# A long convolution's parts placed between panels and heads, a short one halved in PSUM, four low halves on VectorE

## The reference

```
proj = u @ w_in                       # u = x * (1 + scale) + shift
a_in, a_gate, b_in, b_gate, q_lat, kv_lat, k_rope, c_gate, merge_logits = split(proj)
a1, a2 = split(a_in);  a = a1 * sigmoid(a2)
a = causal_depthwise_conv(a, conv_a_w) + conv_a_b          # 31 taps, 512 channels
a = silu(layer_norm(a));  y_a = (a * silu(a_gate)) @ w_a_out
xb, gb, gc = split(b_in)
yb = gb * causal_depthwise_conv(gc * xb, conv_b_w)         # 3 taps, 512 channels
y_b = (yb * silu(b_gate)) @ w_b_out
q = rms_norm(q_lat) @ w_uq;  kv = rms_norm(kv_lat) @ w_ukv # rope on parts of q and k
o = causal softmax attention, 8 heads;  y_c = (o * silu(c_gate)) @ w_c_out
m = sigmoid(merge_logits) gates on y_a, y_b, y_c
out = layer_norm(alpha * x + gate * (m @ w_o))
```

## Time and profile before

| | |
|---|---|
| median of three runs | 1195.85 us |
| the profiled execution | 1201.54 us, span 1199.4 us |
| TensorE busy | 1066.0 us, 89% |
| VectorE busy | 734.1 us, 61% |
| ScalarE busy | 539.8 us, 45% |
| GpSimd busy | 375.3 us, 31% |
| mean granted TensorE clock | 0.930 |
| HBM read | 177.26 MB |
| layer 0: rope_q starts, first xb panel starts, ln_a_mean starts | 582.74, 612.16, 723.60 us |

### The profile page before, as it was taken

How to read it: one execution, slowest core, us unless ns; L and a number is a source line. 1 busy time by engine, 2 the same in 40 slices (tenths; PEclk the granted TensorE clock), 3 DMA queues, 4 the chain that set the end, 5 groups by cost and what they waited for, 6 DMA issues and landing times.

```text
span 1199.4 us, 19568 instructions
## 1 busy us (share of the span) xinstructions
PE 1066.0 (89%) x8104; PEld 994.2 (83%) x8104; DVE 734.1 (61%) x1072; ACT 539.8 (45%) x620; POOL 375.3 (31%) x155
## 2 busy tenths in 40 slices
PE   5989999778799999979977998998789789989985
PEld 4967777578699999968967997998689678979984
DVE  4937887444533422267778597654657875976553
ACT  5543554433444443355533553542574336535432
POOL 3096771000486888501544500000013445000000
PEclk8977999789899999989988999999899898989997
DMA  7632444456565556454533354553637243543601
GB/s 251 194 119 71 143 139 142 137 180 211 159 193 176 176 176 196 157 182 140 172 105 106 115 167 140 189 198 106 186 106 224 85 138 106 176 140 124 205 24 35
DMA packets 159495, 179.56 MB, mean 150 GB/s; under 512 B 5040, under 2 KB 141744, under 8 KB 159408
## 3 DMA queue, kind: packets, MB, share of 16 engines
q1 hardware_dynamic: 159024, 177.22, 46.9%
q0 software_dynamic: 384, 1.10, 0.3%
HBM read 177.26 MB, written 1.05 MB: 149 GB/s over the span
## 4 chain that ended last, share of the span: by engine, by line
PE 62%; DVE 21%; ACT 6%; issue 5%; POOL 3%; DMA 2%; SPq 0%; DVEq 0%; ACTq 0%; POOLq 0%
PE pg L1622 18%; PE pg L1623 18%; PE pg L1624 18%; DVE p_bu L1522 6%; DVE area L1134 4%; DVE area L1138 2%; DVE area L1142 2%; DVE w_lo L1125 2%; ACT w_hi L845 1%; ACT area L823 1%; PE p_s L1712 1%; PE p_s L1616 1%; PE p_y L1778 1%; PE p_o L1812 1%; DVE rows L1170 1%
## 5 line engine op out<-in xcount | busy, mean ns | idle before, releaser
L1622 PE MATMUL pg<-u_hi,w_hi 128*128 128x256 f32 x1664 | 492.2, 296 | 59.7 <-DVE u_lo L1134 37.0
L1623 PE MATMUL pg<-u_lo,w_hi 128*128 128x256 f32 x1664 | 482.5, 290 | 0.0
L1624 PE MATMUL pg<-u_hi,w_lo 128*128 128x256 f32 x1664 | 481.7, 289 | 0.0
L747 POOL TENSOR_TENSOR w_lo<-raw,w_hi 128x2048 fp32r<-128x2048 f32 x62 | 288.3, 4660 | 326.0 <-ACT w_hi L845 326.0
L1622 PEld LDWEIGHTS pg<-u_hi,w_hi 128*128 128x128 f32 x1664 | 331.4, 199 | 70.0 <-issue 64.5
L1623 PEld LDWEIGHTS pg<-u_lo,w_hi 128*128 128x128 f32 x1664 | 332.0, 200 | 0.8
L1624 PEld LDWEIGHTS pg<-u_hi,w_lo 128*128 128x128 f32 x1664 | 331.4, 199 | 0.0
L845 ACT ACTIVATE w_hi<-raw 128x2048 fp32r<-128x2048 f32 (+3 forms) x153 | 275.0, 1804 | 72.7 <-issue 37.4
L1125 DVE TENSOR_TENSOR w_lo<-raw,w_hi 128x2048 fp32r<-128x2048 f32 (+3 forms) x91 | 192.2, 2123 | 84.3 <-ACT w_hi L845 84.0
L851 ACT ACTIVATE area<-pg 128x512 f32<-128x512 f32 (+1 forms) x92 | 54.1, 588 | 178.3 <-PE pg L1624 166.6
L1622 PE MATMUL pg<-vb_hi,w_hi 128*128 128x256 f32 x320 | 91.7, 287 | 5.7 <-issue 3.8
(11 more groups left out here) (201 smaller groups left out, 1355.9 us busy)
## 6 DMA issues: line engine op xcount, KB each, us to landing
raw<-in_w_in SPq DMA_DIRECT2D x68, 1024.0 KB, 5.4
raw<-in_w_ff SPq DMA_DIRECT2D x32, 1024.0 KB, 5.7
raw<-in_w_ada SPq DMA_DIRECT2D x24, 1024.0 KB, 5.2
raw<-in_w_gate SPq DMA_DIRECT2D x8, 1024.0 KB, 7.7
raw<-in_w_o SPq DMA_DIRECT2D x8, 1024.0 KB, 5.1
raw<-in_w_out SPq DMA_DIRECT2D x4, 1024.0 KB, 6.8
raw<-in_w_b_out SPq DMA_DIRECT2D x4, 1024.0 KB, 5.0
raw<-in_w_c_out SPq DMA_DIRECT2D x4, 1024.0 KB, 5.2
```

Source lines behind the costliest of these rows:

```text
L747: pool.tensor_tensor(w_lo[:, s, 0:n], raw[:, r, 0:n], w_hi[:, s, 0:n].bitcast(F32), ALU.subtract).then_inc(sem(f"raw_free{r}"), 1)
L1622: pe.matmul(dst, w_h, x_h, start=first, stop=False)
L1623: pe.matmul(dst, w_h, x_l, start=False, stop=False)
L1624: return pe.matmul(dst, w_l, x_h, start=False, stop=last_)
```

## The change

Three things. The parts of the long convolution stand at other places: part 0 behind a1, 1 behind uq, 2 behind rope_q, 3 between the two cg panels; in the head loop one part at each h but 3 and 4, where before it was h = 0, 1, 2 and 4; one part behind the loop as before; the rest, three instead of five, behind branch1. The short convolution is two steps of two tiles, at h = 3 and h = 4 instead of four tiles at h = 3, and its sums stand in the PSUM bank `p_y` until the last tap. And the low halves of the cg panels are made by VectorE instead of GpSimd. The number of taps and products is the same.

```diff
@@ -67,7 +67,7 @@
-POOL_LOW += [(job, n) for job in ("cg", "xb", "gc", "gb", "bg", "ag") for n in range(2)]
+POOL_LOW += [(job, n) for job in ("xb", "gc", "gb", "bg", "ag") for n in range(2)]
@@ -276,16 +276,20 @@
         step("split", ("ql", l))
         step("split", ("kvl", l))
+        parts = iter(range(2 * CONV_PARTS))
         wide("a1", l, "w_in_2", A1, W)
+        step("conv_a", l, next(parts))
         for n in range(2):
             panel("uq", l, n, "w_uq_2", 0, 4 * QK * n, QL // P, 4 * QK, 2)
+        step("conv_a", l, next(parts))
         panel("ukv", l, 0, "w_ukv_2", 0, 0, KVL // P, 1024, 6)
         step("rope_q", l)
 
-        parts = iter(range(2 * CONV_PARTS))
-        for _ in range(6):
-            step("conv_a", l, next(parts))
-        wide("cg", l, "w_in_2", CG, W)
+        step("conv_a", l, next(parts))
+        for n in range(2):
+            panel("cg", l, n, "w_in_2", 0, CG + 256 * n, KT, 256, 1)
+            if n == 0:
+                step("conv_a", l, next(parts))
...
@@ -298,9 +302,9 @@
-            if h == 3:
-                step("conv_b", l)
-            elif h < 5:
+            if h in (3, 4):
+                step("conv_b", l, h - 3)
+            else:
                 step("conv_a", l, next(parts))
...
@@ -742,7 +746,7 @@
-                    if q["job"] == "cg":
+                    if q["job"] == "xb":
                         pool.wait_ge(*k.last)
...
@@ -1524,12 +1528,14 @@
-            def conv_b(l, _):
-                for j in range(WT):
+            def conv_b(l, half):
+                for j in (2 * half, 2 * half + 1):
                     w = lambda k: col(("conv_b_w", l), 4 * k + j)
-                    ts(bconv[:, j, :], bpad[:, j, 0:T], w(0), None, ALU.mult).then_inc(*c.step())
+                    partial = p_y[:, T * (j % 2):T * (j % 2) + T]
+                    ts(partial, bpad[:, j, 0:T], w(0), None, ALU.mult).then_inc(*c.step())
                     for k in range(1, CONV_B):
-                        stt(bconv[:, j, :], bpad[:, j, k:k + T], w(k), bconv[:, j, :], ALU.mult, ALU.add).then_inc(*c.step())
+                        stt(bconv[:, j, :] if k == CONV_B - 1 else partial, bpad[:, j, k:k + T], w(k), partial,
+                            ALU.mult, ALU.add).then_inc(*c.step())
```

## The result

| | before | after |
|---|---|---|
| median of the runs (range, number) | 1195.54 us (1194.94 to 1198.37, 4) | 1170.80 us (1170.22 to 1171.15, 4) |
| ratio to before, 95% interval | | 0.978 (0.976 to 0.980) |
| profiled execution: time, span | 1201.54, 1199.4 us | 1170.22, 1168.5 us |
| mean granted clock of TensorE | 0.930 | 0.944 |

The kernel is 24.7 us faster by the medians, where 25.85 was forecast (1195.85 to 1170). The ratio is not the quotient of the two medians, which is 0.979 and lies in its interval. The first part of the page of the changed kernel gives each engine's busy time, its share of the span and its instructions.

What follows compares the result with a forecast made beforehand. TensorE bounds the kernel (busy 89%), losing time to waits and low clock: 53.4 us gone, 27.3 new, net 26.1 less, so 1201.54 becomes 1175.4 profiled; the median, 5.7 lower, is predicted as 1170, range 1153 to 1187.

Steps and rivals of the forecast that it cites:

- rope_q's two products: VectorE ahead of the cg reads: 2.4 us instead of 8.7, as GpSimd's pair of low halves is gone.
- half of conv_b: VectorE in heads 3 and 4: two tiles summed in PSUM take 3.0 us, between 2.7 and 7.
- second loop slower than TensorE's, by head 6: Heads 0 to 5: the nmax, exp and low-half loop takes 7.8 us, costing TensorE about 0.4 by head 6.
- wait at turn 6: TensorE waits 5.5 us for normalise 6, behind part 8 and scores 7; 3.3 us of clock follows.
- wait at turn 7, and its time: TensorE waits 1.75 us for normalise 7, so turn 7 is at 678.8 instead of 689.35.
- second slow spell: One shorter low-clock spell of TensorE per layer, 1.7 us, sized as behind the 3.0 us wait.
- wait at merge1 0: From turn 7 to merge1's first low half VectorE has 21.0 us, TensorE 20.0: wait 1.0 us.
- three places: TensorE's waits per layer for bank reads (8.9 us), normalise (6.3 the longest) and the long convolution's end (3.0) go.
- (A): Rival: new waits of heads 6 to 8 don't come, ScalarE's order leaves room; 1144, up to 1155; chance 0.12.
- (B): Rival: heads 0 to 5 don't quite fit, 1 us in each of five heads plus slow clock; 1186; chance 0.15.
- (C): Rival: slower, TensorE waits at every turn, the part lies bare in nine heads; 1211; chance 0.06.
- (D): Rival: cg banks freed late for another reason, spreading brings little; within 3.6 us of 1195.85; chance 0.05.

Runs made afterwards that it cites:

- e1: Changed kernel with the cg low halves made by GpSimd again: 1171.18 us, ratio to before 0.978.
- e8: Kernel before with only the cg low halves moved to VectorE: 1193.31 us, ratio to before 0.996.
- e4: Changed kernel with parts 8 and 9 (heads 6 and 7) moved ahead of the bg bank reads: 1156.86 us, ratio to before 0.966.
- e6: e4 with the bg reads' result in PSUM bank p_y, so bg's product takes one operand from PSUM: 1148.79 us, ratio to before 0.960.
- e7: e6 with the last part ahead of branch1 moved to behind rope_q: 1147.08 us, ratio to before 0.959.
- e2: Changed kernel with six parts in a row behind rope_q again and none in heads 0 and 1: 1186.18 us, ratio to before 0.990.
- e9: Kernel before with conv_b's sums in PSUM, still in one piece in head 3: 1191.14 us, ratio to before 0.994.
- e5: Changed kernel with no part in heads 6 and 7, five behind branch1 instead of three: 1173.19 us, ratio to before 0.980.

## Why the prediction was right, step by step

Steps and sizes for layer 0 (the forecast's clock is that of the trace of before; measured times are the changed kernel's plus the 4.0 us offset, waits and durations as they are):

| step | forecast | measured |
|---|---|---|
| rope_q's two products | 2.4 us | 2.48 us |
| TensorE starts xb 0 | 603.2 | 602.9 (598.89) |
| half of conv_b | 3.0 us | 3.1 us |
| second loop slower than TensorE's, by head 6 | 0.4 us | no wait at turns 1 to 5 |
| wait at turn 6 | 5.5 us | 5.38 us |
| clock behind it | 3.3 us | 3.3 us |
| wait at turn 7, and its time | 1.75 us, 678.8 | 1.79 us, 677.9 (673.94) |
| second slow spell | 1.7 us | 1.7 us |
| wait at merge1 0 | 1.0 us | none |
| wait ahead of ln_a_mean | none | none |

The mechanism was right at each of the three places that the table follows in layer 0, and the row that carried most was the earlier trace rows: it gave rope_q's price with GpSimd out of the way, where the earlier trace rows gave only the price beside it. e1 and e8 confirm the reading from both sides. The two given-back waits came where and, in layer 0, as long as the walk through ScalarE's and VectorE's rows put them.

Three terms were mis-sized, and all are small. The 0.4 us per layer of the longer second loop did not come: the chain's turns at 625.92, 633.64 and 641.36 are TensorE's own 7.7 us apart, and nmax stood for up to 2.2 us in these heads without making TensorE late. I had put that loop at 7.8. GpSimd's low halves start at 604.62, 612.30 and so on to 643.06, which is 7.69 apart, just below TensorE's 7.72. The kernel before had it at 7.70 as well, from the exp at 622.72 to the next at 630.42, so 7.8 was a sum of terms rounded up. The 1.0 us at merge1 0 was counted beside the slow spell of 1.7 just ahead of it. But that spell makes TensorE late, and what it is late by is time VectorE has gained, so the two can't both be paid. Layer 0 of e4, which has no such spell, bears this out and gives the size: there TensorE waits 0.4 us for that low half, not 1.0. And doubling layer 0 left out what layer 1 has more behind turn 7, 0.9 us of wait and 1.7 of clock.

With what was measured, the new terms are 12.2 us in layer 0 (5.38, 3.3, 1.79 and 1.7) and 14.5 in layer 1 (5.25, 3.1, 2.70 and 3.4), so the sum is 53.4 less 26.7, or 26.7 us; the traces show 27.6. The medians show 24.7, and the interval of the ratio (0.976 to 0.980) reaches from 23.9 to 28.5. The 0.9 us between the sum and the traces is about what layer 1 of the kernel before lost more to the clock than layer 0: behind its three waits the mean was 0.65, 0.55 and 0.55 over 7 us each, 8.7 us against the 7.8 that was doubled. That the forecast's 26.1 lies so near is in part luck: two terms that did not come, 2.8 us in both layers, stood against 2.6 us in layer 1 that the doubling missed.

Of the rivals, (A) did not come by itself, since part 8 stood in front of scores 7. But the room that it spoke of was there, 7 us earlier in the same head (idle from 648.69, the part at 655.94): e4, which uses it, takes away 9.9 us of waits, and with e6 and e7 the time ends at 1147 to 1149, inside the range of (A). The argument against it, that turn 7 already waited in the kernel before, holds only for the order of that kernel: in e4 turn 7 still waits 1.27 us, and e6 takes this away with bg's product alone. In the kernel before the product stood behind GpSimd too, in head 6 (1.27 us) and longer in head 7, right ahead of turn 7:

```profile
685.29 2.50 DVE L1134 TENSOR_TENSOR area<-area 128x512 f32<-128x512 f32 x1
```

GpSimd's low half lay there from 682.62 to 687.25. In e6 the same product takes 0.69, so it cost 1.8 us, and turn 7 of the kernel before waited only 0.7. By these rows the product made that wait; no run of the kernel before changes it alone. (B) and (C) needed waits at turns 1 to 5, and there are none. (D) is ruled out by e2: the six parts alone bring back 15.4 us.

In the expectations of the experiments, two missed their range, and e9 and e2 lay on the edge of theirs (1191.14 against 1191 at most, 1186.18 against 1186 at least). e5 missed at the turns: I had allowed them 1 us each at most, and the standing product left 1.8 at each turn of layer 0 and 1.9 at one of layer 1; the 5.7 us at ln_a_mean in layer 0 were inside the 5 to 7 expected. e6 missed by the clock, as told above. What the pieces are worth depends on what else is there (cg low halves 4 us alone and nothing beside the spreading; conv_b's PSUM sums 5.9 us alone and 14.9 when taken away from the changed kernel, where each of the two halves then meets a low half of GpSimd, and the whole conv_b of the kernel before met one). They don't add up to 25, and no run separates them further.

## What to carry to other kernels

When an engine has background work to place, look in the timeline for its idle time ahead of a named release, and put the piece there: two parts of each layer that moved to idle time some 7 us earlier on the same engine took 13.9 us off the time. Where a VectorE operation takes several times what its form takes elsewhere, look for the instruction of GpSimd that ended just before it did, and try one operand or the destination in PSUM before moving work between the engines. When a slow spell of the clock and a wait for another engine stand in a row, count only the longer of the two; this rests on one place, merge1 0. And read every layer's trace before doubling one.

## What the hardware showed that I had not expected

- **How small an operation can stand.** The scaling of a row maximum, 128 x 2 elements, took 2.21 us at 607.05, and ended at 609.26, 0.03 us behind the low half that GpSimd had begun at 604.62 and held for 4.61. Elsewhere it takes 0.17. The reduction ahead of it takes its usual 0.74 for two beside the same low half, and a reciprocal of 128 x 2 in e6 takes its usual 0.17 at 663.58, beside a low half that runs from 659.58 to 664.22. In heads 1 to 6 of layer 0 this scaling is where VectorE meets GpSimd (0.19 to 2.21 us), and turns 1 to 5 come without a wait all the same.
- **PSUM as the way out.** With one operand in PSUM, products and multiply-adds run at 0.69 us (128x512) and 0.48 (128x256) in the middle of a GpSimd low half. The price is small: a multiply with the result in PSUM is 0.49 us against 0.35 in SBUF. The Trainium skill (VectorE: DVE Perf Modes, "Why PSUM operands drop a tier") says that an fp32 operation with an operand in PSUM runs at the single rate only; the two durations agree.
- **The length of a wait of 2 to 3 us doesn't tell what the clock does.** Turn 6 of layer 0 in e4 waits 2.02 us, at 660.54, and the clock stays at 1.00 behind it. Turn 6 of layer 1 in the same execution waits 1.88, at 976.25, and the mean clock behind it is 0.76 (columns as above):

```profile
661.00:668.00 7.00, 6.83 (x53) 6.28 (x52) 6.31 (x11) 5.54 (x6) 4.63 (x1) 1.00 0.13 41
...
976.00:983.00 7.00, 6.75 (x40) 6.07 (x41) 6.19 (x11) 6.35 (x7) 4.60 (x1) 0.76 0.24 81
```

e2 has the same at turn 7: 2.68 us in layer 0 with 1.00 over the 7 us behind it, 2.46 in layer 1 with 0.57 over the 4 us from 1015. In the changed kernel the clock fell behind 5.38 us to 0.53 for some 7 us, which adds 3.3 us to the wait, and waits of 1.79 and 2.70 at turn 7, 12 us behind the long ones, had a second spell behind them. What decides at such lengths is not separated here, so a forecast can take the price of a wait of 5 us from these rows and that of one of 2 to 3 us only as a range, 0 to 3.4.
